# Two of four weight sums of a half-product pair made by accumulating transfers

## The reference

```python
def swiglu(h, w_in, w_out):
    u = h @ w_in                               # 1024 -> 2 x 2816
    gate, up = u[..., :D_FF], u[..., D_FF:]
    return (jax.nn.silu(gate) * up) @ w_out    # 2816 -> 1024

for layer in range(2):
    h = h + 0.5 * swiglu(rms_norm(h, g_ffn1[layer]), w_ffn1_in[layer], w_ffn1_out[layer])
    u = rms_norm(h, g_mix[layer])
    h = h + (attn_mixer(...) if layer % 2 == 0 else pool_mixer(...))
    h = h + 0.5 * swiglu(rms_norm(h, g_ffn2[layer]), w_ffn2_in[layer], w_ffn2_out[layer])
return rms_norm(h, g_final)[:, N_META:]
```

## Time and profile before

| | |
|---|---|
| median of three runs | 1801.53 us |
| the profiled execution's own time | 1801.6 us |
| its span | 1799.5 us |
| mean granted TensorE clock | 0.998 of full speed |
| TensorE busy | 1774.1 us (99%) |
| VectorE busy | 1352.1 us (75%) |
| ScalarE busy | 906.6 us (50%) |
| GpSimd busy | 65.8 us (4%) |
| packets of SyncE's queue, share of 16 DMA engines | 35.2% |

### The profile page before, as it was taken

The page is one execution under the profiler, slowest core; times in us unless marked ns, Lnnn a source line. Parts: engine busy times, 40 slices in busy tenths (PEclk is TensorE's granted clock), DMA queues, the critical chain, the costliest instruction groups (busy, mean ns, idle before and its releaser), DMA issues.

```text
span 1799.5 us, 34396 instructions
## 1 busy us (share of the span) xinstructions
PE 1774.1 (99%) x13812; PEld 1718.9 (96%) x13812; DVE 1352.1 (75%) x1932; ACT 906.6 (50%) x1492; POOL 65.8 (4%) x167
## 2 busy tenths in 40 slices
PE   8999999999999999999999999999999999999998
PEld 8999999999988789999999999999999988899997
DVE  6857998754458866965998789569987678499975
ACT  5434655533247753542655545336555445256555
POOL 0000000021112200200000000000000000000000
PEclk9999999999999999999999999999999999999999
DMA  5242433445454422332433333333342323244332
GB/s 155 82 129 83 113 99 96 106 119 155 160 153 120 129 61 83 95 106 82 113 99 99 90 96 96 115 94 95 101 111 77 100 59 106 83 118 117 96 93 72
DMA packets 335149, 186.96 MB, mean 104 GB/s; under 512 B 18976, under 2 KB 325728, under 8 KB 335008
## 3 DMA queue, kind: packets, MB, share of 16 engines
q1 hardware_dynamic: 331568, 175.63, 35.2%
q0 software_dynamic: 2608, 8.72, 1.2%
q10 hardware_dynamic: 832, 0.62, 0.1%
HBM read 171.51 MB, written 10.82 MB: 101 GB/s over the span
## 4 chain that ended last, share of the span: by engine, by line
PE 91%; DVE 5%; issue 2%; ACT 1%; POOL 0%; DMA 0%; DVEq 0%; SPq 0%; ACTq 0%; POOLq 0%
PE pair L2277 46%; PE pair L2249 17%; PE pair L2218 15%; PE pair L2560 4%; PE pair L779 1%; PE pair L2264 1%; PE pair L2401 1%; PE pair L2488 1%; PE pair L763 1%; PE pair L2434 1%; PE pair L710 1%; PE pair L725 1%; PE pair L733 0%; DVE v_rows L998 0%; PE pair L747 0%
## 5 line engine op out<-in xcount | busy, mean ns | idle before, releaser
L2277 PE MATMUL pair<-b_hi,w_hi 128*128 128x264 f32 (+1 forms) x1344 | 381.8, 284 | 2.6 <-DVE b_lo L1850 1.9
L2277 PE MATMUL pair<-b_hi,w_lo 128*128 128x264 f32 (+1 forms) x1344 | 380.6, 283 | 0.0
L2277 PE MATMUL pair<-b_lo,w_hi 128*128 128x264 f32 (+1 forms) x1344 | 380.5, 283 | 0.0
L2277 PEld LDWEIGHTS pair<-b_hi,w_hi 128*128 128x128 f32 x1344 | 253.2, 188 | 3.7 <-issue 3.5
L2277 PEld LDWEIGHTS pair<-b_lo,w_hi 128*128 128x128 f32 x1344 | 253.4, 189 | 0.0
L2277 PEld LDWEIGHTS pair<-b_hi,w_lo 128*128 128x128 f32 x1344 | 252.9, 188 | 0.0
L2277 PE MATMUL pair<-blocks_hi,w_hi 128*128 128x264 f32 (+1 forms) x816 | 231.8, 284 | 0.8 <-ACT parts L1398 0.8
L2277 PE MATMUL pair<-blocks_hi,w_lo 128*128 128x264 f32 (+1 forms) x816 | 231.3, 283 | 0.0
L2277 PE MATMUL pair<-blocks_lo,w_hi 128*128 128x264 f32 (+1 forms) x816 | 231.2, 283 | 0.0
L1220 ACT ACTIVATE w_hi<-sums_w 128x1024 fp32r<-128x1024 f32 x168 | 177.4, 1056 | 86.4 <-PE pair L2277 44.4
L1220 ACT ACTIVATE w_hi<-raw_all 128x1024 fp32r<-128x1024 f32 (+1 forms) x168 | 142.1, 846 | 138.3 <-PE pair L2277 97.7
(11 more groups left out here) (306 smaller groups left out, 3605.9 us busy)
## 6 DMA issues: line engine op xcount, KB each, us to landing
raw_all<-in_w_ffn_in SPq DMA_DIRECT2D x173, 512.0 KB, 4.1
raw_all<-in_w_ffn_out SPq DMA_DIRECT2D x64, 512.0 KB, 4.3
raw_all<-in_w_ffn_out SPq DMA_DIRECT2D x32, 384.0 KB, 3.7
raw_all<-in_w_attn_in SPq DMA_DIRECT2D x24, 512.0 KB, 4.0
qk_dram<-qk_hi POOLq DMA_DIRECT2D x16, 264.0 KB, 2.3
qk_dram<-qk_lo POOLq DMA_DIRECT2D x16, 264.0 KB, 3.8
raw_all<-in_w_attn_out SPq DMA_DIRECT2D x8, 512.0 KB, 3.9
head_v<-v_tok SPq DMA_DIRECT2D x16, 160.0 KB, 2.6
```

The lines of the kernel that those rows point to most:

```text
L2277: mm = nc.tensor.matmul(dst, w[slot][:, c0 + kk * P:c0 + (kk + 1) * P], rhs(v, kk), start=(fresh and kk == 0 and w is w_hi and v == 0), st ...
```

## The change

GpSimd's queue makes S1 and S3 with transfers between places in SBUF: a copy of block 2 into S1's place, then, when it has landed, two accumulating transfers, block 0 added to block 2 in place in the ring (S3), and block 3 added to S1's place. VectorE keeps S2, now block 2 (which is S3) + block 3, and S4. S2 gets a block of its own just ahead of the ring, so that S2 and S3 can be read by one strided access pattern. S1 and S4 are double-buffered as before. The ring's slots are now held until the low part of S23 is made and S1 has landed; ScalarE's `s14_high` waits for S1 as well. GpSimd runs through all pairs of an FFN in order, before its attention work and after it.

```diff
+        sum2_raw = sb("sum2_raw", [P, 1 + 2 * RING, HALF_K])
+        raw_all = sum2_raw[:, 1:1 + 2 * RING, :].rearrange("p b c -> p (b c)")
...
-        sums_w = sb("sums_w", [P, 6, HALF_K], F32, early)
+        sums_w = sb("sums_w", [P, 4, HALF_K], F32, early)
...
-            def fetch_to(n, j, nk, src, width=P, free=None):
-                if not isinstance(n, int) or n >= RING:
-                    sp.wait_ge(lo_ready, n - RING + 1 if free is None else free)
+            def fetch_to(n, j, nk, src, width=P, of=None):
+                if of is not None:
+                    sp.wait_ge(lo_ready, of.n + 2)
+                    sp.wait_ge(s23_lo, of.s + 1)
+                    sp.wait_ge(s1_done[of.q], sum_number(of))
+                elif not isinstance(n, int) or n >= RING:
+                    sp.wait_ge(lo_ready, n - RING + 1)
...
                 act.wait_ge(s4_done, p.s + 1)
+                act.wait_ge(s1_done[p.q], sum_number(p))
...
-            def weight_sums_13(p):
+            def weight_sum_2(p):
 
-                land_wait(dve, p.n, p.n % RING)
                 land_wait(dve, p.n + 1, (p.n + 1) % RING)
+                dve.wait_ge(s3_done[p.q], sum_number(p))
                 count_ge(dve, s23_lo, p.s)
-                count_ge(dve, s14_lo, p.s - 1)
                 a = raw_pair(p.n)
-                nc.vector.tensor_tensor(s13(p.q), a[:, 0:4:3, :], a[:, 2:3, :].to_broadcast([P, 2, HALF_K]),
-                                        ALU.add).then_inc(s13_done, 1)
+                nc.vector.tensor_tensor(S2, a[:, 2, :], a[:, 3, :], ALU.add).then_inc(s2_done, 1)
...
+            def weight_sums_13(p):
+
+                land_wait(pool, p.n, p.n % RING)
+                land_wait(pool, p.n + 1, (p.n + 1) % RING)
+                count_ge(pool, s14_lo, p.s - 1)
+                a = raw_pair(p.n)
+                pool.dma_start(s1(p.q), a[:, 2, :]).then_inc(s1_copied, 16)
+                pool.wait_ge(s1_copied, 16 * (p.s + 1))
+                pool.dma_start(a[:, 2, :], a[:, 0, :], accum_op=ALU.add).then_inc(s3_done[p.q], 16)
+                pool.dma_start(s1(p.q), a[:, 3, :], accum_op=ALU.add).then_inc(s1_done[p.q], 16)
```

More of the change, by code:

```diff
@@ L319, in trunk @@
         t_lo = sem("t_lo")
-        s13_done = sem("s13_done")
+        s1_copied = sem("s1_copied")
+        s1_done = [sem(f"s1_done{q}") for q in range(2)]
+        s3_done = [sem(f"s3_done{q}") for q in range(2)]
         s2_done = sem("s2_done")
@@ L456, in raw_pair, with s1, s23, blocks_of @@
             return raw_all[:, n % RING * UNIT:(n % RING + 2) * UNIT].rearrange("p (a c) -> p a c", c=HALF_K)
-        def s13(q):
-            return sums_w[:, 1:3, :] if q == 0 else sums_w[:, 1:5:3, :]
+        def s1(q):
+            return sums_w[:, 2 * q, :]
         def s4(q):
-            return sums_w[:, 3 + 2 * q, :]
+            return sums_w[:, 2 * q + 1, :]
         def s14(q):
-            return sums_w[:, 2 + 2 * q:4 + 2 * q, :].rearrange("p a c -> p (a c)")
-        S23 = sums_w[:, 0:2, :].rearrange("p a c -> p (a c)")
+            return sums_w[:, 2 * q:2 * q + 2, :].rearrange("p a c -> p (a c)")
+        S2 = sum2_raw[:, 0, :]
+        def s23(n):
+            at = 1 + 2 * (n % RING) + 2
+            return sum2_raw[:, 0:at + 1:at, :]
+        def blocks_of(w):
+            return w.rearrange("p (a c) -> p a c", c=HALF_K)
+        def sum_number(p):
+            return 16 * (p.s // 2 + 1)
         def a22(w, q):
@@ L1135, in _ @@
                         for p in pairs:
-                            free = pairs[p.head - 2].n + 2 if p.head >= 2 else None
+                            of = pairs[p.head - 2] if p.head >= 2 else None
                             for r in range(2):
@@ L1140, in _ @@
                                     strip(wi, 0, DK, (p.f0 + p.f) * P + r * FF)
-                                fetch_to(p.n + r, (p.n + r) % RING, DK, src, P, free)
+                                fetch_to(p.n + r, (p.n + r) % RING, DK, src, P, of)
                         n1 = n0 + 2 * nf
                         for m in range(DK):
-                            free = pairs[m // 2 - 2].n + 2 if m < RING else None
-                            fetch_to(n1 + m, m % RING, nf, strip(wo, f0 * P, nf, m * P), P, free)
+                            of = pairs[m // 2 - 2] if m < RING else None
+                            fetch_to(n1 + m, m % RING, nf, strip(wo, f0 * P, nf, m * P), P, of)
                 elif ph.kind == "attn":
@@ L1252, in s23_high @@
                 act.wait_ge(s2_done, p.s + 1)
-                copied(w_hi[1][:, :], S23).then_inc(s23_hi, 1)
+                copied(blocks_of(w_hi[1][:, :]), s23(p.n)).then_inc(s23_hi, 1)
             def s14_high(p, prev):
                 act.wait_ge(s4_done, p.s + 1)
+                act.wait_ge(s1_done[p.q], sum_number(p))
                 if prev is None:
@@ L1674, in t_low, with weight_sum_4 @@
                                         t_part(X, 0, i, ph.last), ALU.subtract).then_inc(t_lo, 1)
-            def weight_sums_13(p):
+            def weight_sum_2(p):
+                land_wait(dve, p.n + 1, (p.n + 1) % RING)
+                dve.wait_ge(s3_done[p.q], sum_number(p))
+                count_ge(dve, s23_lo, p.s)
+                a = raw_pair(p.n)
+                nc.vector.tensor_tensor(S2, a[:, 2, :], a[:, 3, :], ALU.add).then_inc(s2_done, 1)
+            def weight_sum_4(p):
                 land_wait(dve, p.n, p.n % RING)
-                land_wait(dve, p.n + 1, (p.n + 1) % RING)
-                count_ge(dve, s23_lo, p.s)
+                dve.wait_ge(s2_done, p.s + 1)
                 count_ge(dve, s14_lo, p.s - 1)
-                a = raw_pair(p.n)
-                nc.vector.tensor_tensor(s13(p.q), a[:, 0:4:3, :], a[:, 2:3, :].to_broadcast([P, 2, HALF_K]),
-                                        ALU.add).then_inc(s13_done, 1)
[L1686 to L1694, removed]
+                nc.vector.tensor_tensor(s4(p.q), S2, raw_pair(p.n)[:, 1, :], ALU.add).then_inc(s4_done, 1)
             def a_low(p):
@@ L1709, in s23_low @@
                 dve.wait_ge(s23_hi, p.s + 1)
-                nc.vector.tensor_tensor(w_lo[1][:, :], S23, w_hi[1][:, :], ALU.subtract).then_inc(s23_lo, 1)
+                nc.vector.tensor_tensor(blocks_of(w_lo[1][:, :]), s23(p.n), blocks_of(w_hi[1][:, :]),
+                                        ALU.subtract).then_inc(s23_lo, 1)
             def s14_low(p):
@@ L1932, in plain_dve @@
                 gate_out(ph, n - 4)
-                weight_sums_13(p)
                 weight_sum_2(p)
@@ L1971, in pair_dve @@
                     hid_low(A, p.keeper, lo)
-                if nxt is not None:
-                    weight_sums_13(nxt)
                 if plain and prev is None:
@@ L2657, in _ @@
                                     pattern=[[-1, P]], channel_multiplier=1).then_inc(consts2, 1)
+            def weight_sums_13(p):
+                land_wait(pool, p.n, p.n % RING)
+                land_wait(pool, p.n + 1, (p.n + 1) % RING)
+                count_ge(pool, s14_lo, p.s - 1)
+                a = raw_pair(p.n)
+                pool.dma_start(s1(p.q), a[:, 2, :]).then_inc(s1_copied, 16)
+                pool.wait_ge(s1_copied, 16 * (p.s + 1))
+                pool.dma_start(a[:, 2, :], a[:, 0, :], accum_op=ALU.add).then_inc(s3_done[p.q], 16)
+                pool.dma_start(s1(p.q), a[:, 3, :], accum_op=ALU.add).then_inc(s1_done[p.q], 16)
             for ph in PHASES:
+                if ph.kind == "ffn":
+                    for _, _, _, _, _, pairs in ph.blocks:
+                        for p in pairs:
+                            weight_sums_13(p)
                 if ph.kind != "attn":
```

1 line of the change is left out of this document (removed).

## The result

The changed kernel takes 1974.53 us (median of 4 runs, 1970.03 to 1976.0) against 1801.27 us before on the same chip (4 runs): a ratio of 1.0958, 95% interval 1.0939 to 1.0977. That is 173 us more, where 12 were forecast and the top of the range stood 48 above the kernel before.

What follows compares the result with a forecast made beforehand. TensorE, 91% of the chain that ended last, was taken to bound the kernel. Chain starts cost 7.0 + 5.4 us, less 0.7 gained: 11.7 us on 1801.6, so 1813 us, with a range of 1802 to 1850.

Steps and rivals of the forecast that it cites:

- next to nothing to win: TensorE's waits inside the seven-product chains were 3.3 us in all; the gain was put at 0.7 us.
- the issues on GpSimd: Three issues a pair at 0.54 us, 1.6 us in a pair of 10.2; the queue is not the limit.
- the second rival, the ring as the bound: Adding transfers need over 4.1 us even without company: 1849 at 5.0 us, 1890 at 6; chance 0.26.
- the steady ring, cost 0: Late in a chain, release to S3 takes 11.4 us; VectorE waits 1.0 us, still starts S2 0.3 earlier: cost 0.
- the chain starts: At a chain's third pair S3 lands late: 3.5 us at two starts, 1.35 at four, 7.0 + 5.4 us.
- I take 2.3 for the copy, as no fetch runs then: GpSimd's copy into S1's place lands 2.3 us after issue, 2.5 with semaphore waits.
- 3.1 for the addition: S3's accumulating transfer lands about 3.1 us after issue when alone, used for the steady pairs.
- half a pass, as the 4.3 assumed: S3's addition beside a fetch takes 4.3 us: half a data pass over the plain transfer's 3.8; used at chain starts.
- Every microsecond costs half a microsecond a pair: Beyond the about 12.4 us the ring carries, each us costs half a us a pair; one release serves the pair after next.
- the later release: Ring slots are released at the end of S23's low part (L1710) instead of block 3's low part (L1704).

Runs made afterwards that it cites:

- x7: The changed kernel with SyncE's fetches for a pair held back until S3 of the pair before has landed: 1995.23 us.
- x6: The changed kernel without GpSimd's copy; SyncE fetches block 2 a second time from HBM straight into S1's place: 1813.3 us.
- x13: The changed kernel with GpSimd's three transfers a pair cut to 64 of 512 columns, so most sums are incomplete: 1845.95 us.
- x1: The changed kernel with three S1 buffers instead of two, so the copy waits for an earlier pair's `s14_low`: 1932.62 us.
- x2: The changed kernel with VectorE's order changed: `s14_low` and the next pair's `a_low` ahead of S2, S4 after the gating: 1877.8 us.
- x5: The changed kernel with both accumulating transfers made plain copies, so sums S1 and S3 are left out: 1897.84 us.
- x3: The kernel before, sums still on VectorE, with fetches also waiting for the low part of S23: 1801.37 us.
- x9: The changed kernel with x6's second fetch in place of the copy and x2's order on VectorE: 1805.28 us.

## Why the prediction was wrong

Right: that there was next to nothing to win (at most 3.3 us); that the copy alone takes 2.3 us (x7) and the addition alone 3.1 (3.3 in x7 and as the least of the change); that the issues on GpSimd (0.57, 0.84, 1.17 us) do not bind; that the cost is paid before S2. The direction held. The case that came true is the second rival, the ring as the bound, priced at 1849 to 1890 with a chance of 0.26; even it was 85 us short.

The step that failed is **the steady ring, cost 0**: the pairs away from the chain starts were to cost nothing, and with the copy taken out of their line (x6) 161 of the 173 us came back. The step stood on four supports, and three gave way:
- "I take 2.3 for the copy, as no fetch runs then", and 3.1 for the addition. SyncE's releases follow VectorE's order, not GpSimd's, and fall on the addition as soon as VectorE is late: 57 of the 84 additions had packets of a fetch beside them and landed after 4.9 us at the median, 26 of them after more than 5. Packets of S3 issued at 224.89 began only at 228.8, as the next pair's fetch ran from about 225.2 to 229.9 (times of single packets in the trace), while an addition alone has its first packet after 1.4 us. So this transfer was not slowed by half a pass, as the 4.3 assumed, but held back by half of the fetch and more; 16 of the 84 had their first packet after more than 3 us. The rows of L2685, 3.6 to 5.0, were too mild a neighbour. x7 shows the 3.3 without company, x13 that bytes carry 129 us.
- The ring was followed over two pairs only, with half a us a pair for each us of excess. The one-pair cycle was overlooked: S2, S4, `s14_low` of the pair before take 2.6 us, the copy that waits for it 2.6, S3 4.3 to 6.6, then S2: 9.5 to 11.8 us, on both sides of the 10.2 us of a pair, and here an excess counts in full in each pair in which the copy waits for that low part, 30 of 84 in the change; in most others it waits for the fetch, in the longer cycle. The 168.7 us are 2.0 a pair: pairs now take some 12.2 on average. Its two links were cut in x1 (42 us) and x2 (97 us, which shortens the other cycle too), and the copy taken out of S3's line in x6. The prediction had listed `s14_low` behind S2 on VectorE, and did not ask what on GpSimd waits for it: `count_ge(pool, s14_lo, p.s - 1)` stands in the diff.
- "Every microsecond costs half a microsecond a pair" left TensorE's clock out. 24 stretches at the lower level came with waits of 1.6 to 6.2 us, an estimated 45 us in all. x5 and x13 (69.8 and 29.6 us of half clock for 73 and 36 us of waits) show the two falling together, but not in step: x7 has more waits than the change (135) and less half clock (101).

The fourth, the later release, held as far as it was tested: with the sums on VectorE it costs nothing (x3). In the changed kernel it was not tested by itself.

The Trainium skill, "DMA: Bandwidth & Descriptors", section "Issuing engines are not separate DMA queues", speaks of all issuers' transfers sharing the 16 DMA engines and interleaving. The trace agrees on the sharing: additions beside a fetch landed after 4.9 us at the median, alone after 3.3. How evenly they interleave the passage doesn't say; here a 256 KB transfer got no packet for 3.9 us from its issue, 2.5 more than alone, while the 1 MB fetch ran.

The chain starts (12.4 us forecast) can't be told apart in a trace in which most pairs are late. In x6 and x9, where most of the rest is steady, 12 and 4 us remain. In x9 TensorE's 8.7 us of waits in the pairs fall in eight places: four on the u4 copy (4.7 us), each within the first five pairs of a chain, and four on the hidden tile's low part (4.0 us, where it was 1.9). So something like the forecast cost of the starts is there, but smaller. Open, too, is how the loss divides exactly: x1 and x2 remove parts of one loop, and their gains don't add (42 and 97 alone, 101 together). Nor was the clock's share measured by a run of its own.

## What to carry to other kernels

When a sum moves from an engine to a chain of transfers, write down every cycle through the buffers it touches, one pair long and two pairs long, and give each transfer the time it takes beside the largest fetch of the kernel, since being late makes it meet that fetch. Before an in-order engine is made to wait for a landing, move ahead of it what does not need the landing (97 us here for three moved calls); and a transfer that only prepares a place for an addition should come straight from the source with the fetch, not in line behind it (161 us). Idle time on an engine that does not bind is worth nothing: 102 us of VectorE were freed, and no version was faster.

## What the runs showed of the hardware

- A 256 KB addition between places in SBUF takes 3.3 us from issue to landing when alone, against 2.3 for a copy; with packets of a fetch beside it, 3.3 to 7.4 and 4.9 at the median. A copy in its place also took up to 7.2 (x5).
- A transfer of GpSimd can wait long for its first packet while a fetch of the other queue runs: 3.9 us after the issue of an addition at 224.89, and over 3 us for 16 of 84, against 1.4 for an addition alone (1.1 for a copy).
- TensorE's clock: 126 us at 1.2 GHz in 25 stretches, 24 of them in or just after waits of 1.6 to 6.2 us, in a kernel whose TensorE is busy 93%; an estimated 45 us of the 169 (a matmul each 0.22 instead of 0.12 us).
- A second read of 256 KB from HBM per pair, beside the same additions, left the kernel 4 us above the one before (x9, 1805.3 us).
